# Layer 1 of a hybrid decoder step: tile 1's output and expert choice placed between its mixer and the sample's mixer

## What is computed

```python
for li in range(DEPTH):
    hm = _rmsnorm(x, norm1_g[li]) * (1 + sc1) + sh1
    out, S = _rwkv7_mix(hm, ...) if li % 2 == 0 else _gla_mix(hm, gla_S, ...)
    x = x + gt1 * out
    hc = _rmsnorm(x, norm2_g[li]) * (1 + sc2) + sh2
    x = x + gt2 * _peer(hc, peer_wq[li], peer_subkeys[li], peer_u[li], peer_v[li])
y = _rmsnorm(x, final_g)

def _peer(...):    # 8 heads, 16 of 128 x 128 experts each
    q = xt @ wq;  s = q . subkeys                  # scores
    i1, i2 = top_k(s)                              # expert = i1 * 128 + i2
    act = gelu(take(u, expert) . xt)               # key rows
    return sum(gate * act * take(v, expert))       # value rows
```

## Time and profile before

| what | value |
|---|---|
| median of 3 runs | 2972.89 us (2957.26 to 2974.44) |
| the profiled execution's own time | 2963.4 us |
| its span, first to last instruction | 2961.6 us |
| PE, DVE, POOL busy | 1884.3, 1596.7, 1276.4 us |
| moved by DMA | 828.08 MB, mean 280 GB/s |
| of that, gathered rows (queue q0) | 604.05 MB |
| mean granted TensorE clock | 0.790 |

### The profile page before, as it was taken

How to read it: one execution, slowest core, us unless ns; L and a number is a source line. 1 busy time by engine, 2 the same in 40 slices (tenths; PEclk the granted TensorE clock), 3 DMA queues, 4 the chain that set the end, 5 groups by cost and what they waited for, 6 DMA issues and landing times.

```text
span 2961.6 us, 25805 instructions
## 1 busy us (share of the span) xinstructions
PE 1884.3 (64%) x9717; PEld 1172.2 (40%) x9717; DVE 1596.7 (54%) x2986; ACT 275.6 (9%) x434; POOL 1276.4 (43%) x1160
## 2 busy tenths in 40 slices
PE   5879857837868766657667767678455675023433
PEld 2459523327845335454245337363223353000100
DVE  4253376575842736868312146865766218974333
ACT  1111000010110010010100110001110000000000
POOL 0000012543543555655334235557656234477674
PEclk8889979967879887667788878789677897556677
DMA  8430586964679896867999868789879687699997
GB/s 274 171 130 2 192 302 209 360 229 141 220 264 339 296 328 231 266 203 245 344 343 339 310 234 324 266 290 386 294 273 362 231 309 286 243 403 410 409 409 317
DMA packets 296711, 828.08 MB, mean 280 GB/s; under 512 B 45951, under 2 KB 57135, under 8 KB 296589
## 3 DMA queue, kind: packets, MB, share of 16 engines
q0 software_dynamic: 165888, 604.05, 55.4%
q1 hardware_dynamic: 120132, 218.02, 21.0%
q10 hardware_dynamic: 10568, 4.38, 0.6%
HBM read 816.05 MB, written 10.31 MB: 279 GB/s over the span
## 4 chain that ended last, share of the span: by engine, by line
PE 31%; DVE 24%; DMA 22%; POOL 10%; issue 7%; ACT 3%; PEld 1%; SPq 0%; ACTq 0%; DVEq 0%; POOLq 0%; PEldq 0%
PE psum L1918 29%; POOL arena L709 7%; DMA arena<-in_peer_v,idx_v 7%; DVE arena L1095 7%; DVE arena L1115 6%; POOL wring L709 4%; DMA wring<-in_ada_w 2%; DMA wring<-in_peer_v,idx_v 2%; DMA wring<-in_gla_w_in 2%; DMA wring<-in_rw_w_rkv 2%; DMA wring<-in_peer_wq 1%; DMA out<-arena 1%; PE psum L1936 1%; DVE hc L1095 1%; DVE hT L1095 1%
## 5 line engine op out<-in xcount | busy, mean ns | idle before, releaser
L709 POOL DMA_INDIRECT arena<-in_peer_u,idx_u x476 | 597.2, 1255 | 993.1 <-DVE acts L1115 441.4
L1918 PE MATMUL psum<-arena 128*32 128x512 f32 (+6 forms) x3666 | 628.7, 588 | 434.1 <-DMA arena<-in_peer_v,idx_v 223.8
L709 POOL DMA_INDIRECT arena<-in_peer_v,idx_v x428 | 432.6, 1011 | 558.7 <-PE psum L1918 398.0
L1918 PEld LDWEIGHTS psum<-arena 128*32 128x32 f32 (+2 forms) x3666 | 321.3, 172 | 672.4 <-issue 551.8
L1115 DVE CUSTOM_DVE_ANT_0 arena<-arena,hc 128x1024 f32<-128x1024 f32 x396 | 469.1, 1225 | 84.0 <-DMA arena<-in_peer_u,idx_u 46.9
L1918 PE MATMUL psum<-wring,arena 128*32 128x512 f32 (+3 forms) x808 | 231.3, 700 | 118.7 <-DMA wring<-in_peer_v,idx_v 75.8
L1918 PE MATMUL psum<-pick,ident 128*128 128x256 f32 x906 | 231.6, 413 | 43.9 <-DVEq L1366 36.1
L1918 PEld LDWEIGHTS psum<-pick,ident 128*128 128x128 f32 x906 | 183.4, 208 | 116.4 <-issue 45.1
L1918 PE MATMUL psum<-wring,hT 128*128 128x512 f32 (+1 forms) x480 | 191.2, 557 | 16.4 <-DMA wring<-in_gla_w_in 12.9
L1918 PEld LDWEIGHTS psum<-wring,arena 128*128 128x128 f32 (+2 forms) x808 | 90.1, 173 | 250.8 <-issue 225.7
L1918 PE MATMUL psum<-hT,wring 128*128 128x128 f32 (+3 forms) x1312 | 177.1, 297 | 12.9 <-DMA wring<-in_peer_wq 6.1
(11 more groups left out here) (227 smaller groups left out, 1857.2 us busy)
## 6 DMA issues: line engine op xcount, KB each, us to landing
wring<-in_ada_w SPq DMA_DIRECT2D x24, 2048.0 KB
wring<-in_peer_wq SPq DMA_DIRECT2D x20, 2048.0 KB
wring<-in_rw_w_rkv SPq DMA_DIRECT2D x12, 2048.0 KB
wring<-in_gla_w_in SPq DMA_DIRECT2D x12, 2048.0 KB
wring<-in_rw_wo SPq DMA_DIRECT2D x6, 2048.0 KB
vring<-mod_d SPq DMA_DIRECT2D x22, 512.0 KB
wring<-in_gla_wo SPq DMA_DIRECT2D x4, 2048.0 KB
arena<-in_peer_u,idx_u POOLq DMA_INDIRECT x476, 6.4
```

Source lines behind the costliest of these rows:

```text
L709: pool.indirect_dma_start(slot(s, n), None, v_rows if side else u_rows, bass.IndirectOffsetOnAxis(index, 0)).then_inc(rows_landed[s], 16)
L1918: return nc.tensor.matmul(out, lhsT, rhs, start=start, stop=stop)
```

## The change

Layer 1's order becomes: `gla_mixer((1, SAMPLE))` with the projections of both but `gla` only for tile 1; `out(1, (1,))`; `gla(SAMPLE)`; `out(1, (SAMPLE,))`; the rest. The sample gets its own pass over output weights, keys and queries. Tile 0's rounds are no longer mingled: its 32 key rounds come first, and its 32 value rounds (176 to 207) run in `out(1, (1,))` on groups 0, 1 and `LENT`, whose four slots now are arena and hidden-row space. Of tile 1, the first 64 key columns are in `gla(SAMPLE)`; its later key rounds and first value rounds stay mingled, in `out(1, (SAMPLE,))`. Groups 2 and 3 come in from round 256 on (208 before). Tile 1's hidden rows stay in SBUF (`hc`); only the sample's are copied to PSUM. Tile 1's choice has a desk of its own in the arena, the gate weights of the second mixer move to `hT`, and state buffers move too.

```diff
-MINGLED = ((1, 0), (1, 1))
+MINGLED = ((1, 1),)
...
-LATE_AT = round_at(1, 1, 0, 0)
+LATE_AT = round_at(1, 1, 1, 16)
...
-LENDINGS = ((round_at(1, 0, 0, 16), round_at(1, 0, 1, 16)),)
+LENDINGS = ((round_at(1, 0, 1, 0), round_at(1, 1, 0, 0)),)
...
+        slots += [C(1), C(2), hc[:, 0, :], hc[:, SAMPLE, :]]
...
+            def gla_out(t):
                 keys(1)
+                for k in (2, 4, 3):
+                    mod_vec(1, k, t == SAMPLE)
                 queries(1)
...
+            gla_gate_weights((1, SAMPLE))
+            gla_weights(range(7))
+            vec(row("gla_gnorm"))
+            out_weights(a["gla_wo"][0])
+            gla_out(1)
+            mod_vec(1, 5)
+            vec(row("gla_gnorm"))
+            out_weights(a["gla_wo"][0])
...
+            sp.wait_ge(region_free, w.next(region_free))
+            load_state(0)
+            sp.wait_ge(gla_space, 1)
+            load_state(1)
+            for h in range(2):
+                store_state(h)
+                sp.wait_ge(gla_state_stored[h], 16)
+                load_state(h + 2)
+            for h in (2, 3):
+                store_state(h)
+            gla_out(SAMPLE)
...
-            RATES = {"mix": 14, "core1": 1.9, "core2": 4.0, "enter": 6, "gla": 2.4, "out": 7}
+            RATES = {"mix": 14, "core1": 1.9, "core2": 4.0, "enter": 6, "gla": 2.6, "out": 7, "last": 8}
...
             def hidden(li, t):
-                return psum[:, (t - 1) * D:t * D] if li and t else hc[:, t, :]
+                return psum[:, 0:D] if li and t == SAMPLE else hc[:, t, :]
...
-                    open_rows(1, 0, 64, 64, RATES["gla"], True)
-                for t in tiles:
-                    gla(t, tiles)
+                    open_rows(1, 0, 64, 64, RATES["gla"])
+                gla(tiles[0], tiles)
+                dve.sem_inc(region_free, 1)
                 if tiles[0]:
-                    weights_due(1, 0, 1)
+                    rest_rows()
+                    dve.sem_inc(lent_space, 1)
...
+                if li and t == SAMPLE:
+                    open_rows(1, 1, 64, 64, RATES["last"], True)
+                gated_add(t, add_tmp)
...
+                    if li and t < SAMPLE and half == 0:
+                        weights_due(*((0, SAMPLE), (1, 0, 1))[t])
...
+                if t == SAMPLE:
+                    if li:
+                        rest_rows()
+                        weigh(1, 1, 1)
                     for m in range(4):
+                        top16(d.top_s[:, 0, m, :], d.top_i[:, 0, m, :], sample_scores[:, m, :], d.rest[:, 0:P])
+                    choose(li, SAMPLE, 0, PH // COPIES)
+                    if li:
+                        build(1, 1, 1)
+                if li and t == 1:
+                    add_experts(1, 0, add_tmp)
...
+            open_rows(1, 1, 0, 64, RATES["gla"])
+            gla(SAMPLE, (1, SAMPLE))
+            dve.sem_inc(region_free, 1)
+            weights_due(1, 1, 0)
+            out(1, (SAMPLE,))
             last_norm(0)
...
-            VALUE_RATES = {"out": 0.5, "gla": 0.5, "mingled": 0.6, "core2": 0.8}
+            VALUE_RATES = {"out": 0.5, "gla": 0.5, "last": 2, "core2": 0.8}
...
                 if t0:
                     fan_weights(1, 0, 0)
-                    open_values(1, 0, VALUE_RATES["mingled"], 16, 0, True)
...
-                for t in tiles:
-                    gla(t, tiles)
+                gla(t0, tiles)
                 if t0:
-                    rest_values()
-                    buffer_back(lent, round_at(1, 0, 1, 16))
-                    fan_weights(1, 0, 1)
-                    open_values(1, 0, 0, 16, 16)
+                    open_values(1, 0, 0)
...
-                        if SAMPLE in tiles:
-                            rounds_now(2 if li else 1)
+                        rounds_now({(0, SAMPLE): 1, (1, 1): 2}.get((li, tiles[0]), 0))
...
             for tiles in ((0,), (1, SAMPLE)):
                 gla_mixer(tiles)
-                out(1, tiles)
+                out(1, tiles[0:1])
+            gla(SAMPLE, (1, SAMPLE))
             fan_weights(1, 1, 0)
-            open_values(1, 1, 0, 16)
-            rest_values(0)
+            open_values(1, 1, VALUE_RATES["last"], 16, 0, True)
+            out(1, (SAMPLE,))
             fan_weights(1, 1, 1)
```

More of the change, by code:

```diff
@@ L1 @@
+from collections import namedtuple
 from contextlib import ExitStack
@@ L374, in program, with desk, desk_of @@
         onehot = cand
[L375 to L380, removed]
+        Desk = namedtuple("Desk", "top_s top_i dealt sc pf e1 e2 pos pi rest iF")
+        def desk(top, small, rest):
+            part = [small[:, P * i:P * (i + 1)] for i in range(7)]
+            return Desk(top[:, 0:512].rearrange("p (t i e) -> p t i e", t=2, i=HP),
+                        top[:, 512:1024].bitcast(U32).rearrange("p (t i e) -> p t i e", t=2, i=HP),
+                        *part[0:5], part[5].bitcast(U32), part[6].bitcast(U32), rest[:, 0:256], rest[:, 256:512])
+        usual_desk, other_desk = desk(C(10), C(11), C(12)), desk(C(4), C(9), C(3))
+        def desk_of(li, t):
+            return other_desk if li and t == 1 else usual_desk
         sample_scores = C(12)[:, 512:1024].rearrange("p (n k) -> p n k", n=4)
@@ new lines, in _ @@
+            gla_weights(range(5))
+            gla_gate_weights((0,))
+            gla_weights(range(5, 7))
+            vec(row("gla_gnorm"))
+            mod_vec(0, 5)
+            out_weights(a["gla_wo"][0])
+            gla_out(0)
+            mod_vec(0, 5, True)
+            for t in (1, SAMPLE):
+                for k in (1, 0):
+                    mod_vec(1, k, t == SAMPLE)
+            gla_gate_weights((1, SAMPLE))
+            gla_weights(range(7))
+            vec(row("gla_gnorm"))
+            out_weights(a["gla_wo"][0])
@@ L1549, in gla @@
                 ps = fill()
+                if sample:
+                    dve.sem_inc(gla_space, 1)
                 ts(b["la"], ps[:, 0:512], 0.0, None, ALU.min)
@@ L1588, in gla @@
                     done(dve.memset(qem, 0.0))
-                    for h in (1, 0, 3, 2):
+                    for h in range(GH):
                         done(dve.tensor_copy(diag_blocks(qem), own_rows(qe[:, h * P:(h + 1) * P])))
@@ L1904, in weight @@
                 return b
-            def buffer_back(b, end):
-                for j in range(GRP):
-                    pe.wait_ge(rows_used[GRP * LENT + j], lent_uses(end))
-                pe.sem_inc(weight_used[b], 1)
             def release(b, s, n):
@@ L2387, in out @@
                     release(b, psum_for_vector, nfv[0])
-                if tiles[0]:
+                if tiles[0] and not (li and tiles[0] == SAMPLE):
                     rounds_now(4 if li else 1)
```

163 lines of the change are left out of this document (53 added, 110 removed).

## The result

| what | before | after |
|---|---|---|
| median | 2965.56 us (2957.26 to 2974.44, 4 runs) | 3017.82 us (3006.61 to 3025.55, 4 runs) |
| ratio | 1 | 1.0174 (95% interval 1.0148 to 1.0200) |
| span of the profiled execution | 2961.6 us | 3023.7 us |
| moved by DMA | 828.08 MB | 841.78 MB |

The kernel became slower by 1.7%. Timed once more beside the last experiments, its ratio was 1.0143 (1.0121 to 1.0165). The median of before stands on four executions here; the forecast was made against three (2972.89 us).

A forecast was written before the change was run, and what follows sets the result against it. Bound by slots and order of work up to 2543 us, by transfers after it. Round 260 starts 53 us later: 2963.4 + 53 = 3016, or 3026 set against the median; taken as 3018, range 2942 to 3072.

The forecast's parts named there:

- The deciding step: Sample's output and choice: sixteen value rounds go singly through one four-slot group; round 260 starts at 2845, 53 us later.
- the ring: Alternating rounds: 13 value rounds of 13.5 us (issue 3.7, landing 6.3, TensorE 2 to 3.2, release 0.8), 176 us, to 2821.
- its steps from 2561 to 2645: Sample's output: weights and vector to 2573, a value round to 2592, product and norm to 2618, keys and queries to 2643.
- Rival (b): Key rows read from SBUF slow gather issue: about 2.5 us more a round, 33 us, time 3050; chance 0.16.
- Rival (a): Value rounds run at GpSimd's pace: 13 x 10.0 = 130 us instead of 176, time 2972, no change; chance 0.21.
- (c): Early start wins: at 340 GB/s from 2403 to round 256 it breaks even, at 380 it ends at 2925; chance 0.13.
- Tile 1's mixer: From 2073: own work 38, all 64 row products 74, idle 9, so 121 us, ending at 2194.
- Tile 1's output and choice: After 2194: 32 value rounds of tile 0 at 5.05 us, 162 us; round 208 starts at 2403, VectorE free at 2408.
- The sample's mixer: Mixer of the sample alone: own work 46, 64 products 74, idle 33, so 153 us, to 2561.
- the sample's output: Stage after the sample's mixer, from 2561: gated add and norm done by 2618, first value round by 2645.
- the choice: After the sample's keys, done about 2815: gelu 4, top 16 and choice 19 us, two builds, to 2841.
- What is added: Sample's own pass over output weights, queries and keys: 13 MB, 33 us at 400 GB/s, hidden in slot waits, no term.

The follow-up runs named there:

- the third group: Changed kernel plus a third group of four slots for rounds 224 to 255, so value rounds are not bound to one: 2973.37 us, ratio 1.0024 to the kernel before.
- 11 MB less: Changed kernel loading only an eighth of each of the sample's six added output and query weight blocks: 3007.14 us, ratio 1.0129 to the kernel before.
- keys first: Changed kernel without mingling: tile 1's later key rounds run alone, all 32 value rounds behind them on sixteen slots: 2958.93 us, ratio 0.9978 to the kernel before.

## Why the prediction was right

**The deciding step held.** The prediction said that all sixteen value rounds pass through one group of four slots, at 13.5 us each, and that 260 starts 53 us later than before. It started 59.7 later, and 208 to 260 took 438.1 us against 2845 - 2403 = 442. The trace shows the ring at its place, and the third group took 42 of the 131 us by which this distance had grown, 38 of them in the alternating rounds. So the mechanism and the direction are shown. The other large part, 65 us between 224 and 232, the forecast had in its steps from 2561 to 2645 (84 us; measured 2560 to 2644.6), but no run took it away.

**How much of it is luck.** Forecast 3018 us, measured 3017.8. That they agree to a microsecond is chance: before's median was taken as 2972.9 and is 2965.6, so the step up was forecast as 45 us and measured as 52 (43 in the second timing), and several errors of 10 to 14 us in the steps cancelled (below). The lower end of the range does not follow from its own terms either: 3018 less 46 and 20 is 2952, not 2942.

**The ring, term by term.** The forecast had thirteen rounds, 231 to 255, of 13.5 us from 2645 on, so that TensorE has used the last at 2821. They began at 2644.6, and the last was used at 2834.6:

```profile
2831.09 3.48 PE L1920 MATMUL psum<-arena 128*32 128x512 f32 x16 [7.90 <-DMA arena<-in_peer_v,idx_v]
```

That is 190 us instead of 176, 14.6 a round: each was priced about 1.2 short. In the mean of the twelve full turns, issue took 4.43 us where the forecast had 3.7, landing 6.6 where it had 6.3 (one landing took 10.9, in a turn of 19.3 us), and TensorE's use with the release 3.7 where 3.5 was kept. In the turn shown, TensorE's round took 3.64, above the 2 to 3.2 allowed, and the release 0.22, below the 0.8. So the issue was mis-sized most; in the turn shown it was 4.76, because the first gather took 1.97 us.

**Rival (b) is inside that term.** The gathers of the decisive stretch in after (2645 to 2826, duration in ns, min/median/max):

```profile
L721 POOL DMA_INDIRECT arena<-in_peer_v,idx_v x52: 933/938/1987, 2644.6 to 2824.8; - x52
L721 POOL DMA_INDIRECT arena<-in_peer_u,idx_u x48: 933/937/1292, 2649.6 to 2816.2; - x48
```

The medians say that nothing is at work. The single ones say otherwise. Of the 52 value gathers 31 lie beside a row product of VectorE, which now reads a gathered row and the hidden row both in SBUF, and these took 1.35 us in the mean (20 of them were lengthened, 11 were not); the 21 others took 0.94. For the turn shown, VectorE's row products are

```profile
2776.64 1.23 DVE L1125 CUSTOM_DVE_ANT_0 arena<-arena,hc 128x1024 f32<-128x1024 f32 x1
...
2777.86 1.23 DVE L1125 CUSTOM_DVE_ANT_0 arena<-arena,hc 128x1024 f32<-128x1024 f32 x1
```

and the gather of 1.97 us starts at 2776.70, as the first one has begun. Over the stretch the lengthening is 12.7 us (11.0 in the second profile of after), about 1.05 a turn, where rival (b) had 2.5. A median hides an effect that strikes one or two gathers in a turn, and each of them delays the last gather of the turn. In before, with the hidden row in PSUM, 87 key gathers beside row products between 208 and 260 took 0.945 in the mean. The Trainium skill, SBUF — State Buffer, section "Who interferes with whom", says that a VectorE instruction with two inputs in SBUF contends with a GpSimd instruction that reads SBUF, and that the port pair which they share is an exclusive lock. The trace agrees in that gathers were lengthened only beside such products (0.94 us in all 21 others, 0.945 with one input in PSUM), but 11 of the 31 beside one kept their 0.94 us. Whether after without this effect would gain all 12.7 us was not tried: it would need a place in PSUM for tile 1's hidden row.

**Rivals (a) and (c) fell.** Rival (a) wanted 10.0 us a turn; the shortest of the twelve took 12.1. From 208 to 256 after moved 293 GB/s, as the sum had it (296), below the 340 from which the order would break even. In (c) the early start was to hide the ring; the early start is there (71.5 us), the ring takes it back and 60 us more.

**Steps that were off and cancelled.** Tile 1's mixer ended at 2196.4, forecast 2194, but it began 6 us late (2079.4), which no step had foreseen, and took 117 instead of 121. Tile 1's output and choice ended with the experts added at 2421.1, not at 2408: 224.7 us for 214. GpSimd waited 65.2 us there for TensorE to use value rows, in 16 waits, and the transfers were near full (366 GB/s, DMA share 0.94), so the issue at 5.05 us a round was the wrong limit. The first indices came at 2335.7, 78 us before 208, as estimated. The sample's mixer took 139 us, not 153: I kept 33 us of idle time and 19 were there (119.93 busy of 139). VectorE's waits for TensorE's heads in it:

```profile
DVE arena L1608 <- PE psum L1920: 12.1, 4, 3.5
```

Before they were 21.2 us in the same four waits, with a further 6.4 for a state. The state's wait is gone. A likely reason for both is that no value round stands on TensorE between the heads now, but this was not tried; the forecast kept both waits as they were. Late by 13 ahead of the mixer and 14 quicker in it, the sample's output started on its forecast: norm by 2616.8 (2618), the alternating rounds from 2644.6 (2645). The ring ended 13.5 us late, but the choice does not wait for value round 255, only for the last key rows. They were used at 2823.6, 8.6 us late (2815): round 254 is issued behind value round 253, its last gather started at 2816.2 and had still to land. Then the choice took 19.4 us (2825.7 to 2845.1) as forecast, and 260 started at 2852.0, 7 us later than forecast.

**What is added.** The trace shows 13.7 MB more, forecast 13. "It lies in the slot waits" held to within what was measured: 11 MB less gave 1 to 3 us from 208 to 260, and 4 to 13 us by the ratios.

## What to carry to other kernels

Where two streams alternate and slots are dealt out by round number, count the slots of each stream, not of both: with two groups and a strict alternation each stream has one, and it runs as a ring of issue, landing, use and release, whose terms add up. Three groups, or one stream at a time, broke the ring; starting TensorE's product earlier didn't.

Measure an order by the distance between two fixed points in it (here rounds 208 and 260), beside the whole time: in the two profiles of after it agreed to 2 us where starts differed by 12. One profile is not enough for a small effect, though: keys first without and with the third group were 15 us apart in it, with equal medians. And split the distance: the same stretch held the ring and, ahead of it, 65 us of another kind.

## What was not expected of the hardware

A row product with both inputs in SBUF lengthened a gather beside it from 0.94 to as much as 1.99 us, yet with sixteen slots ahead of the transfers this cost 11 us in all by the ratio (20 by one profile), and in the ring of four slots the gathers grew by 12.7 us of 176. And thirty to forty such gathers don't show in a median: in the stretch where it mattered the median was 938 ns.
